# Decoder step with expert retrieval: the convolution's steps spread over the expert pairs, its norm in two parts, two stores placed later

## The reference, cut to what matters

```
h = rmsnorm(x) @ w_in                    # u_a, v_a, val_b, gate_b, q_m and three gates
y_a = gelu(u_a) * (tril(ws) @ layernorm(gelu(v_a)) + b)      # chunks of 128 rows
glu = val_b * sigmoid(gate_b)
ext = concatenate([conv_past, glu])      # 30 rows of the past in front; its last 30 are an output
c = causal_depthwise(ext, 31 taps) + b   # channel by channel
y_b = silu(layernorm(c))
y_m = attention(q_m, 256 memory rows)
x = x + (sig(gA)*(y_a@w_o_a) + sig(gB)*(y_b@w_o_b) + sig(gM)*(y_m@w_o_m)) @ w_out
# experts: product keys give 16 of 16384 experts for each row and each of 8 heads
hid = gelu(dot(rmsnorm(x), u_tab[eid]))
x = x + sum over the 128 picks of gate * hid * v_tab[eid]
```

## Time and profile before

| what | value |
|---|---|
| median of 3 executions | 2237.01 us (2234.17 to 2238.07) |
| the profiled execution | 2238.65 us, span 2236.9 us |
| mean granted TensorE clock | 0.813 of full |
| busy: TensorE, VectorE, GpSimd, ScalarE | 73%, 70%, 32%, 29% of the span |
| DMA | 895.56 MB, mean 400 GB/s |
| gathers / other transfers | 604.02 MB / 289.54 MB |
| convolution steps (L1143) | 960 instructions, 275.2 us |
| dot products (L1672) | 576, 687.4 us |

### The profile page before, as it was taken

How to read it: one execution, slowest core, us unless ns; L and a number is a source line. 1 busy time by engine, 2 the same in 40 slices (tenths; PEclk the granted TensorE clock), 3 DMA queues, 4 the chain that set the end, 5 groups by cost and what they waited for, 6 DMA issues and landing times.

```text
span 2236.9 us, 31355 instructions
## 1 busy us (share of the span) xinstructions
PE 1631.0 (73%) x10944; PEld 1069.0 (48%) x10944; DVE 1567.8 (70%) x4170; ACT 656.0 (29%) x1647; POOL 721.5 (32%) x660
## 2 busy tenths in 40 slices
PE   9999987788797477878788647766999853334334
PEld 9866675566675055554433415543887610000002
DVE  4464269988766667877775577787876686776775
ACT  3121232421414242432132323342223332322222
POOL 0000056332232433342222234531323254454443
PEclk9999998899898588999899757876999865555556
DMA  9699899999899999999999999999999999999997
GB/s 338 250 385 402 335 406 420 384 418 400 327 410 419 422 420 421 422 412 422 421 390 421 421 421 414 409 393 396 420 417 421 409 400 421 422 421 421 422 421 317
DMA packets 127773, 895.56 MB, mean 400 GB/s; under 512 B 16096, under 2 KB 16928, under 8 KB 20480
## 3 DMA queue, kind: packets, MB, share of 16 engines
q0 software_dynamic: 83232, 604.02, 65.6%
q1 hardware_dynamic: 44384, 289.54, 32.1%
HBM read 885.39 MB, written 8.11 MB: 399 GB/s over the span
## 4 chain that ended last, share of the span: by engine, by line
PE 33%; DMA 28%; DVE 24%; issue 4%; ACT 4%; DVEq 3%; POOL 3%; SPq 0%; POOLq 0%; ACTq 0%
DMA uv<-uv_in,idx_u 22%; PE bank L1797 14%; DVE uv L1672 11%; PE bank L2109 5%; PE bank L2453 4%; DMA ring<-w_in 4%; DVE yB L1143 3%; PE bank L1803 3%; POOL uv L611 2%; DMA ring<-cache_in 2%; POOL merged L638 1%; ACT L675 1%; DVEq L1138 1%; ACT diag L1036 1%; DVE x L1695 1%
## 5 line engine op out<-in xcount | busy, mean ns | idle before, releaser
L611 POOL DMA_INDIRECT uv<-uv_in,idx_u x574 | 652.1, 1136 | 1294.5 <-PE bank L2453 634.1
L1672 DVE CUSTOM_DVE_ANT_0 uv<-uv,xrep 128x1024 f32<-128x1024 f32 x576 | 687.4, 1231 | 217.0 <-DMA uv<-uv_in,idx_u 209.6
L2453 PE MATMUL bank<-uv,diag 128*32 128x512 f32 x2176 | 393.0, 803 | 476.2 <-ACT diag L1036 470.3
L1797 PEld LDWEIGHTS bank<-xnT,ring 128*128 128x128 f32 x3168 | 434.5, 202 | 77.4 <-issue 68.3
L1797 PE MATMUL bank<-xnT,ring 128*128 128x160 f32 (+1 forms) x3168 | 456.2, 304 | 1.1 <-DMA ring<-w_in 1.0
L675 ACT ACTIVATE pick<-pick 128x2 f32<-128x2 f32 (+1 forms) x315 | 66.9, 213 | 1053.3 <-DVE pick L1672 1052.5
L2453 PEld LDWEIGHTS bank<-uv,diag 128*32 128x32 f32 x2176 | 49.4, 122 | 663.3 <-ACT diag L1036 598.0
L1143 DVE SCALAR_TENSOR_TENSOR yB<-ext_p,small,yB 128x128 f32<-128x128 f32 x960 | 275.2, 348 | 19.5
L675 ACT ACT_TABLE_LOAD x137 | 175.8, 1283 | 2.4
L1036 ACT ACTIVATE diag<-gated_fold,pick 128x32 f32<-128x32 f32 x574 | 153.1, 314 | 9.8 <-ACT pick L675 0.5
L2109 PE MATMUL bank<-ring,xnT 128*128 128x512 f32 x192 | 88.3, 615 | 0.0
(11 more groups left out here) (323 smaller groups left out, 1848.0 us busy)
## 6 DMA issues: line engine op xcount, KB each, us to landing
ring<-w_in SPq DMA_DIRECT2D x211, 1024.0 KB
uv<-cache_in SPq DMA_DIRECT2D x16, 1024.0 KB, 9.6
ring<-cache_in SPq DMA_DIRECT2D x16, 1024.0 KB
uv<-uv_in,idx_u POOLq DMA_INDIRECT x578, 13.9
uv<-w_in SPq DMA_DIRECT2D x4, 1024.0 KB, 10.3
ring<-w_in SPq DMA_DIRECT2D x6, 512.0 KB, 4.7
ext_s<-state_in SPq DMA_DIRECT2D x2, 1088.0 KB, 14.0
convs_out<-ext_s SPq DMA_DIRECT2D x2, 1088.0 KB, 24.7
```

The lines of the kernel that those rows point to most:

```text
L611: nc.gpsimd.indirect_dma_start(out=uvbuf[2 * b + i], out_offset=None, in_=uv_in, in_offset=bass.IndirectOffsetOnAxis(ap=ids[:, c:c + 1], a ...
L1672: ins = V.tensor_tensor_reduce(out=u, in0=u, in1=xrep[gg % 2][:, :], scale=1.0, scalar=0.0, op0=ALU.mult, op1=ALU.add, accum_out=hid[:, c: ...
L1797: ins = MM(out, w[:, k, P * b:P * (b + 1)], rhs(k), start=k == 0, stop=k == KB - 1)
L2453: ins = MM(vbank[gg % 2][c:c + 32, :], diag[:, t % 4, i], uvbuf[2 * b + i][:, D + 512 * n:D + 512 * (n + 1)], start=first, stop=last)
```

## The change

It has three parts, all for the odd portions, 1 and 3.

1. The convolution's steps are no longer called at places of the mixing. `TAPS[m][u]` says how many steps are to be done by pair u, and VectorE calls `conv_upto` with it in every pair of an even portion, behind the picking and (where k is 2 or 4) behind the first call of the stepper, ahead of the last one. A step is done only once the four pieces `glu` of its half are there. The steps are spread by weights, `HEAVY`, over k = 0 to 7, from the first pair whose reach takes in glu4 to two pairs before the one that reaches csum: pairs 4 to 32 in portion 1 and u = 8 to 36 in portion 3. The counts in `gated`, `beside` and at va3 go for odd portions; `conv(2 * CONV_W)` ahead of `centre` stays, to finish what might be left.
2. In odd portions `norm_c` yields once more, at place mg14, between the scaling and the wait for the root. In portion 1 this is the pair after csq, u = 37 in place of 36; in portion 3 both places are reached in u = 40.
3. SyncE's wait for the eighth glu and its two stores stand behind the load of va2 and no longer behind that of q3, three pieces later.

```diff
+HEAVY = (1, 1, 3, 3, 4, 3, 1, 1)
+
+def taps_by(m):
+    us = range(PAIRS * STEPS[(m - 1) % 2])
+    first = next(u for u in us if reach(m, u - 1) >= PLACE[m]["glu4"])
+    last = next(u for u in us if reach(m, u - 1) >= PLACE[m]["csum"]) - 2
+    total, so_far, out = sum(HEAVY[u % PAIRS] for u in range(first, last + 1)), 0, []
+    for u in us:
+        so_far += HEAVY[u % PAIRS] if first <= u <= last else 0
+        out.append(-(-2 * CONV_W * so_far // total))
+    return out
+
+TAPS = {m: taps_by(m) for m in range(1, PORTIONS, 2)}
...
-                    if p == 1 and (kind, i) == ("q", 3):
+                    if p == 1 and (kind, i) == ("va", 2):
                         sp.wait_ge(S["glu"], at("glu", m, 8))
...
-                done = [0]
+                done, glued = [0], [0]
...
+                def conv_upto(n):
+                    while done[0] < n and glued[0] >= 4 * (done[0] // CONV_W + 1):
+                        conv(1)
+
+                if p:
+                    beside_pair[0] = conv_upto
...
+                    glued[0] = c + 1
...
                 def beside(name, taps):
                     yield place[name]
-                    conv(taps)
+                    if p == 0:
+                        conv(taps)
...
-                    if m == 1:
-                        conv(2)
...
-                def gated(first, last, taps):
+                def gated(first, last):
...
-                        conv(taps)
...
-                        conv((2, 1, 2, 0)[m])
+                        conv((2, 0, 2, 0)[m])
...
                     V.tensor_scalar(rb[:, 0:nt], t_bank[:, 0:nt], 1.0 / D, EPS, ALU.mult, ALU.add).then_inc(S["cvar"], 1)
+                    if p:
+                        yield place["mg14"]
                     dve.wait_ge(S["rt_c"], at("rt_c", m, 1))
...
-                    taps = 1 if m in CACHED else 2
-                    yield from gated(0, 3, taps)
+                    yield from gated(0, 3)
...
-                    yield from gated(8, 12, 3 if m in CACHED else 4)
+                    yield from gated(8, 12)
                     conv(2 * CONV_W)
...
+                    if m % 2 == 0:
+                        beside_pair[0](TAPS[m + 1][u])
                     if mix:
                         mix(reach(m + 1, u - 1))
```

More of the change, by code:

```diff
@@ L1478, in mixing @@
                 else:
-                    taps = 1 if m in CACHED else 2
-                    yield from gated(0, 3, taps)
+                    yield from gated(0, 3)
                     yield from norm_v_gain()
-                    yield from gated(3, 5, taps)
+                    yield from gated(3, 5)
                     yield from norm_v_bias()
-                    yield from gated(5, 8, taps)
+                    yield from gated(5, 8)
                     yield from spatial()
-                    yield from gated(8, 12, 3 if m in CACHED else 4)
+                    yield from gated(8, 12)
                     conv(2 * CONV_W)
                     yield from centre()
-                    yield from gated(12, 14, 0)
+                    yield from gated(12, 14)
                     yield from norm_c()
-                    yield from gated(14, 24, 0)
+                    yield from gated(14, 24)
                 for i in range(4):
@@ L1736, in layer @@
                 return next(i for i in range(PORTIONS) if s < FIRST[i + 1]) // 2
+            beside_pair = [None]
             V.memset(one, 1.0).then_inc(one_set, 1)
```

## The result

The changed kernel takes **2254.9 us** (median of 5 executions, 2253.43 to 2255.88) against 2235.87 for the kernel before in the same comparison: ratio 1.0083, 95% interval [1.0068, 1.0098], 19 us slower. The forecast was 2236.1, the range ended at 2247. The profiled execution took 2253.64 us, span 2251.9.

The account below looks back on a forecast made before the run. DMA transfers were taken as the bound, starved by VectorE where they idle; first layer -1.5 us and second +0.6 gave -0.9 on the profiled 2238.65, forecast against the median as 2236.1 us, range 2227 to 2247.

Parts of the forecast that it names:

- the old lump near the end: Second layer, 1570 to 1670: transfers already run at 420 GB/s, so the old lump of steps there costs nothing.
- Forecast for the second layer: Later requests, contention and the vanished stall give 1.6 us more idle time at 1450 to 1470, 1.0 won later: net +0.6.
- The 15.5 us given back: First layer behind 530: of 16.7 us idle transfer time, all but 1.2 us is won back.
- The norm, which had a range of 0 to -3.7 us: First layer, 580 to 632: splitting the norm saves 0 to 3.7 us, adding nothing as that idle time is already counted.
- The steps and their delay: First layer: eleven more steps, 13.2 us, ahead of pair 18, less 1.2 hidden plus 2.0 contention: 14.0 us later.
- Contention: Pairs 4 to 8: GpSimd's multiplications slow VectorE's steps by 2.0 us, of which 1.2 in pair 4; bounds zero and 12.8.
- Rival 2: Pairs 4 to 8: every multiplication blocks VectorE, 12.8 us in place of 2.0; 2246.9 us, chance 0.22.
- 430 to 450 was to grow to some 19 us: First layer: sign that the forecast is right, the idle stretch at 430 to 450 grows to some 19 us, ending near 456.
- Rival 1: Pairs ahead of 18: early steps hide in VectorE's 6.6 us idle time, pair 18 only 6.6 later; 2227.5 us, chance 0.29.
- TensorE's 5.82 us stall: Second layer, until 1453.04 ahead of va0: goes once the stores follow the loads, taking 5.8 us off.
- rival 3: Second layer, near 1473: a late store holds GpSimd's memset and gathers 5 to 6 us; near 2241.5 us, chance 0.06.
- idle time behind 530 or pairs 7 us apart there: First layer: sign against the forecast, idle time staying behind 530 although pairs are 7 us apart, making TensorE the bound.

Follow-up runs that it names:

- the late counts at the new place: Kernel before with portion 3's old counts up to u = 23 and the changed kernel's counts and place of steps from there: 2245.42 against 2235.32 us.
- the run with portion 1's two edits alone: Kernel before with portion 1's steps counted and the norm in two parts, stores at the old place: 2242.76 against 2235.32 us.
- the faster version: Kernel before with portion 1's old counts to u = 17, 44 steps spread over u = 18 to 32 ahead of the waits, norm split: 2228.86 against 2235.62 us.

## Why the prediction was wrong

**The term that failed: "From 1570 to 1670 the engines run at 420 GB/s, and the old lump near the end costs nothing".** This stretch was put at nothing and cost 8.9 us of idle transfers (from 0.5 to 9.4 in 1570 to 1680). That the old lump cost nothing was true. That steps put there would cost nothing did not follow. The row itself showed TensorE busy 96.5 of 100 us: it kept up with little to spare. The new counts put 26 steps at u = 26 to 36, the old ones 18: 8 x 1.2 = 9.6 us more of VectorE's queue ahead of the products that TensorE's next work waits for. And the steps stood behind the products, which uncovered 4.6 us of waiting in pair 180 alone with the old counts (6.8, 5.35 and 1.45, in the changed kernel). The chain of pairs loses 23.4 us from pair 170 to 181 in the changed kernel (7.3 come back by pair 184), 14.4 with the steps ahead of the waits, and 6.4 with the old counts at the new place; the two causes together give about the whole. In the time of the kernel the place is the larger as far as the runs divide them: the late counts at the new place cost 9 to 10 us, the old counts at that place 8 to 9, with intervals that overlap, so by themselves the late counts add some 1 us; early and late counts together bring it to 14. From 1650 to 1670 the changed kernel shows the transfers running dry and TensorE short of work:

```profile
1650.00:1660.00 10.00, 6.90 (x27) 5.16 (x27) 7.30 (x22) 2.53 (x7) 3.04 (x2) 0.54 0.86 335
1660.00:1670.00 10.00, 10.00 (x71) 8.99 (x71) 5.13 (x17) 0.61 (x2) 1.88 (x2) 0.95 0.75 292
```

Forecast for the second layer +0.6 us; measured by the shift from pair 143 to pair 287 11.8, by the idle transfers 19.5 - 8.8 = 10.7. For the first it was -1.5 us; the idle transfers give +2.1, pair 143 +3.1, and the run with portion 1's two edits alone 7 by its median.

**The second fault: the change was costed by which pair a step is in, and never by where in the pair it stands.** The diff says plainly that `conv(taps)` goes from ahead of the wait in `gated` into one block, behind the stepper's first call where k is 2 or 4 and ahead of its only call elsewhere. No term of the sum stands for that. The prediction asked for waits that the early steps might use, but not for waits that the old steps already used. The rows of before show no bracket at L1364 in those pairs, and that was read as no wait. Runs with the old counts at the new place put it at 7 to 9 us in each portion; the changed kernel with its steps back ahead of the waits gets 11 to 12 of its 19 us back.

**The 15.5 us given back.** 13.3 us came back (16.7 less 3.4), with the norm split; without it less, since the stretch 580 to 632 then moves 396 GB/s and with it 416. The norm, which had a range of 0 to -3.7 us and nothing in the sum, had a share in it after all: alone it gave nothing, beside the counted steps of portion 1 the time fell from 12 to 7 us over the kernel before. What a shortening is worth depends on what else stands in the chain: this one gave nothing in the kernel before, some 5 us beside the counted steps, and perhaps 2 in the faster version.

**What held, in part by luck.** The steps and their delay: pair 18 came 13.9 us later, forecast 14.0 (13.3 if the 0.6 by which pair 4 was late already is taken off). Its parts were off both ways. Contention was put at 1.2 us in pair 4 and 2.0 in all; in pair 4 alone it was some 2: pair 5 comes 7.9 or 8.0 us later against pair 4, where five steps are 6.0. But by pair 8 the shift has grown by 11.4 us, less than the 12.0 of the ten steps done by then, so more than the 1.2 us of waits that the sum had taken hid under them. Rival 2, 12.8 us of contention, had the right sign for another reason. The prediction found no row with a convolution step beside a multiplication; the changed kernel has one, at 330.10. VectorE paid there, 2.24 - 1.12 = 1.1 us on tap 0 and 5.53 - 4.78 = 0.75 on the block behind it, which began 1.15 us before the multiplications' end (330.88 + 2.70); these took 2.70 us against 2.57 alone. Single instructions of tap 0 last up to 0.72 us there and 0.34 elsewhere. For the four multiplications 1.1 + 0.75 us make 0.47 each, between the 0.3 that the sum took and its upper bound of 0.64. Beside two dot products and a selection it is GpSimd that pays more, 4.70 us for four.

The Trainium skill, SBUF — State Buffer, section Who interferes with whom, calls what the two engines share an exclusive lock, for which a VectorE instruction with two SBUF inputs contends with a GpSimd instruction that reads SBUF. The rows agree that each holds the other up; the sum at its upper end, which that rule seemed to ask for, did not come, since up to pair 8 only one group of four multiplications met steps.

The place of the idle time was not as forecast: 430 to 450 was to grow to some 19 us and has 2.6, while 5.6 stand at 323 to 360 and 7.6 at 450 to 530. Rival 1 fell with pair 18. The stores: TensorE's 5.82 us stall went, as forecast, but its worth of 5.8 us did not arrive; moving them either way changes nothing in the time, so the stall may have lain under something else. That the memset would suffer (rival 3) was not seen. Up to 1570 the second layer cost 10.1 - 8.3 = 1.8 us, near the +0.6 of the forecast.

**What would have shown it.** The prediction's last part named idle time behind 530 or pairs 7 us apart there as signs against it. It had no sign for the second layer behind 1570 at all, which is how a stretch costed at nothing goes unwatched.

**Still open.** The 6 to 8 us that remain with the steps ahead are put down to the new counts of both portions together, steps taken too early and too few left at the gates of pairs 31 and 180; how they divide was not tried. The share of the split norm in the faster version is not settled. Why the removed va0 stall brought nothing was not followed: with the stores moved alone, 1410 to 1500 moves 410 GB/s in place of 397, 2.8 us less of idle transfers, and the time is the same.

## What to carry to other kernels

Work that stands ahead of a wait covers it, and a trace then shows no wait: before moving filler, take it out in thought and ask what its engine would stand for. Move it first with its amounts unchanged, then change the amounts; here the two together lost 19 us, where milder counts in portion 1 with the steps ahead of the waits, and the norm split, won 7. A stretch in which the transfers are full may still hang on an engine that is busy 97% of it, and more work ahead of that engine is not free.

## What had not been expected of the hardware

Which engine pays for a meeting of GpSimd and VectorE depends on what meets. Four multiplications beside two dot products and a selection take 4.70 us in place of 2.57, and a dot product beside them 1.68 in place of 1.22. Beside convolution steps they take 2.70, and there the steps pay: four instructions of tap 0 take 2.24 us in place of 1.12.

From 360 to 430 the DMA engines show a busy share of 1.01 at 391 GB/s, and from 1450 to 1460 one of 1.03 at 274:

```profile
1450.00:1460.00 10.00, 7.84 (x45) 6.66 (x46) 9.09 (x30) 5.12 (x12) 1.88 (x2) 0.83 1.03 274
```

Ahead of the prediction a share of 1.01 was called full; it is no proof of full speed. These stretches hold the two stores, and in other kernels the slow stretch moves with them. The changed kernel issues them at 384.65 and 1449.90, and 380 to 390 and 390 to 400 move 375 and 291 GB/s. With the stores back behind q3 the first pair of them is issued at 368.66, and the slow stretch is this:

```profile
370.00:380.00 10.00, 4.58 (x21) 2.62 (x22) 8.36 (x17) 2.29 (x5) 8.24 (x10) 0.66 1.03 284
```

With the stores alone moved they are issued at 1436.66, and 1440 to 1450 moves 336 GB/s at 1.04. In the kernel before the first layer's stores, issued at 356.31, take until 380.32 to land and the rate stays at 416 or more, so it also matters what else is under way. In the time of the kernel none of this showed.

Last, TensorE's clock. In the changed kernel it was granted 0.54 of full from 1650 to 1660, so the lower of its two levels nearly throughout, a stretch in which TensorE had stood 2.24 us for ScalarE and 1.85 for VectorE. The kernel before has such a dip too, somewhat later and shorter: 0.75 and 0.57 in 1655 to 1660 and 1660 to 1665, TensorE busy 1.66 of the first 5 us. By stretches of 5 us, 1650 to 1665 lacks 5.1 us of full clock in the changed kernel and 3.4 in the one before. So what TensorE's waits around pair 180 add is a little to a dip that was there; what it costs was not measured.
